# Sample attention of a decoder step: two batches side by side on 128 partitions, token rows kept in DRAM meanwhile

## The reference, cut to what matters

```python
def _sb_attend(q, k, v, mask, sb_bias):
    z = jnp.einsum('bqhd,bkhd->bhqk', q, k) * (q.shape[-1] ** -0.5)
    z = z + sb_bias[None, :, None, None]
    log_1m = jnp.where(mask, jax.nn.log_sigmoid(-z), 0.0)
    excl = lax.cumsum(log_1m, axis=3, reverse=True) - log_1m
    a = jnp.where(mask, jnp.exp(jax.nn.log_sigmoid(z) + excl), 0.0)
    return jnp.einsum('bhqk,bkhd->bqhd', a, v)

def _dilated_sample(q, k_buf, v_buf, rel_bias):
    ...
    for window, dil in DILATED_PATTERNS:     # (128,1), (512,4), (2048,16)
        idx = lb + jnp.arange(t)[:, None] - dil * m[None, :]
        kg, vg = jnp.take(k_buf, idx, axis=1), jnp.take(v_buf, idx, axis=1)
        logits = jnp.einsum('bthd,btmhd->bhtm', q32, kg) * scale + bias.T[:, None, :]
        lse = jax.nn.logsumexp(logits, axis=-1)
        outs.append(jnp.einsum('bhtm,btmhd->bthd', jnp.exp(logits - lse[..., None]), vg))
        ...
    return _combine_dilations(outs, lses)
```

## Time and profile before

| | |
|---|---|
| median of three runs | 2693.51 us |
| span of the profiled execution | 2693.6 us |
| sample attention in it (870.56 to 1733.90 us) | 863.3 us |
| TensorE busy | 2265.2 us, 84% |
| VectorE busy | 1438.1 us, 53% |
| ScalarE busy | 1021.5 us, 38% |
| GpSimd busy | 816.8 us, 30% |
| mean granted TensorE clock | 0.909 |
| moved by DMA | 371.71 MB |

### The profile page before, as it was taken

One profiled execution on the slowest core, in us unless ns is written; L12 is line 12 of the kernel. 1 busy time (PEld: TensorE's weight loads), 2 busy tenths in 40 slices (PEclk: granted clock), 3 DMA queues, 4 the chain that ended last, 5 costly groups with the idle time before them and its releaser, 6 DMA issues. The chain is left out here.

```text
span 2693.6 us, 42705 instructions
## 1 busy us (share of the span) xinstructions
PE 2265.2 (84%) x15058; PEld 2062.9 (77%) x15058; DVE 1438.1 (53%) x1784; ACT 1021.5 (38%) x1582; POOL 816.8 (30%) x401
## 2 busy tenths in 40 slices
PE   5999955776666788888888898577999999999998
PEld 4999934555555677767776776477899999999997
DVE  5111128898986587877787887475522212222213
ACT  3000015767666455556555555421301211111212
POOL 2211104333340254553553543411222221122210
PEclk7999977878888798988898998789999999999999
DMA  3222175212210676666666766510444334433332
GB/s 114 98 85 84 65 280 144 67 47 57 65 48 26 194 242 200 221 212 209 211 212 211 226 203 219 176 36 32 141 141 141 124 109 140 140 128 137 108 124 105
DMA packets 183929, 371.71 MB, mean 138 GB/s; under 512 B 38289, under 2 KB 71442, under 8 KB 182674
## 3 DMA queue, kind: packets, MB, share of 16 engines
q1 hardware_dynamic: 178130, 289.64, 34.2%
q0 software_dynamic: 5056, 79.96, 8.3%
q10 hardware_dynamic: 624, 0.80, 0.2%
HBM read 339.07 MB, written 98.11 MB: 162 GB/s over the span
## 5 line engine op out<-in xcount | busy, mean ns | idle before, releaser
L1406 POOL TENSOR_TENSOR sa_v_lo<-sa_v_in,sa_v_hi 128x1536 fp32r<-128x1536 f32 (+2 forms) x104 | 341.0, 3282 | 436.8 <-ACT sa_v_hi L1602 342.1
L393 POOL TENSOR_TENSOR mlp_w_lo<-mlp_raw,mlp_w_hi 128x2048 fp32r<-128x2048 f32 x30 | 138.2, 4606 | 585.7 <-ACT mlp_w_hi L439 585.7
L1666 DVE TENSOR_TENSOR sa_kT_lo<-sa_kt,sa_kT_hi 128x512 fp32r<-128x512 f32 (+1 forms) x352 | 211.2, 653 | 144.1 <-ACT sa_kT_hi L1564 143.8
L1467 PE MATMUL sa_s<-sa_kT_hi,sa_qd 128*128 128x512 f32 (+1 forms) x704 | 246.4, 414 | 3.7 <-DVE sa_kT_lo L1666 3.7
L552 DVE TENSOR_TENSOR xT<-xT,mlp_acc 128x1088 f32<-128x1088 f32 x64 | 82.4, 1287 | 278.8 <-PE mlp_acc L144 278.8
L962 PE MATMUL pr_turned<-ident,pr_take 128*128 128x128 f32 x576 | 100.2, 306 | 140.2 <-DVE pr_wtsT L1145 127.4
L1444 PE MATMUL sa_kt<-ident,sa_k_in 128*128 128x128 f32 x1344 | 177.3, 289 | 42.6 <-DMA sa_k_in<-in_cache_sb_k 21.6
L1564 ACT ACTIVATE sa_kT_hi<-sa_kt 128x512 fp32r<-128x512 f32 (+1 forms) x352 | 174.9, 570 | 100.2 <-PE sa_kt L1444 100.2
L1444 PEld LDWEIGHTS sa_kt<-ident,sa_k_in 128*128 128x128 f32 x1344 | 166.3, 150 | 55.6 <-DMA sa_k_in<-in_cache_sb_k 22.7
L962 PEld LDWEIGHTS pr_turned<-ident,pr_take 128*128 128x128 f32 x576 | 68.6, 153 | 166.2 <-issue 166.0
L144 PE MATMUL mlp_acc<-n_hi,mlp_w_hi 128*128 128x272 f32 x1024 | 171.8, 290 | 21.0 <-POOL mlp_w_lo L120 16.3
(11 more groups left out here) (193 smaller groups left out, 5237.8 us busy)
## 6 DMA issues: line engine op xcount, KB each, us to landing
sa_k_in<-in_cache_sb_k SPq DMA_DIRECT2D x256, 256.0 KB, 3.5
sa_v_in<-in_cache_sb_v SPq DMA_DIRECT2D x256, 256.0 KB
out<-in_cache_win_k POOLq DMA_DIRECT2D x16, 2040.0 KB, 8.7
out<-in_cache_win_v POOLq DMA_DIRECT2D x16, 2040.0 KB, 8.6
sa_k_in<-in_cache_win_k SPq DMA_DIRECT2D x80, 256.0 KB, 4.3
sa_v_in<-in_cache_win_v SPq DMA_DIRECT2D x80, 256.0 KB
mlp_raw<-in_w_up SPq DMA_DIRECT2D x16, 1024.0 KB, 11.5
mlp_raw<-in_w_down SPq DMA_DIRECT2D x16, 1024.0 KB, 11.0
```

The source lines that it names most:

```text
L393: pool.tensor_tensor(out=ring.lo[:, n % 2, :], in0=ring.raw[:, n % 2, :], in1=ring.hi[:, n % 2, :].bitcast(F32), op=ALU.subtract).then_inc ...
L1406: last = pool.tensor_tensor(out=v_lo[0:rows, h, i, :], in0=v_in[0:rows, s, i, :], in1=v_hi[0:rows, h, i, :].bitcast(F32), op=ALU.subtract)
L1467: last = pe.matmul(out[:, 0:w], qd[:, k, qp, c * P:(c + 1) * P], kT[:, n % 2, c, 0:w], start=(c == 0 and x == 0), stop=(c == PAIRS - 1 and ...
L1666: dve.tensor_tensor(kT_lo[:, n % 2, c, 0:w], kt_ps[:, c, 0:w], kT_hi[:, n % 2, c, 0:w].bitcast(F32), ALU.subtract).then_inc(kT_lo_done, 1)
```

## The change

`sample_stage` now takes two batches at a time (G = 2), four turns in place of eight. Their 2 x 64 rows lie side by side on the 128 partitions of the scores, of the two sigmoids, the scan, the product, the softmax and the transposed weights, so that these are one instruction for two batches. Keys and values of the two batches stay apart: the queries of batch g stand in columns g x 64 of `qd[..., g, ...]`, with zeros elsewhere, and all eight (batch, head pair) products of a unit add up in one accumulator. Values go to one accumulator per batch.

A step, one unit of both batches, is cut into eight slots j (batch j // 4, head pair j % 4). In each slot every engine does one eighth of each kind of work: TensorE transposes the keys of a slot three ahead, scores this slot, and multiplies one tile of values of the unit four steps back. Sigmoids stand in slot 0 of the next step, scan and product in slots 1 and 2, value halves of two tiles in slots 2, 3, 5 and 6, weights in slots 6 and 7 three steps after their scores; `own_heads` and `place` have slots of their own. Key and value buffers are three instead of two, `kT` six slots, `v_hi` and `v_lo` six halves. GpSimd makes all of `v_lo`. The new tokens' keys, before a product of their own, are loaded as eight more rows of a unit; the unit of new tokens alone is now two pages and the new tokens, and the last unit two pages. There are 42 tiles per batch as before.

The tables on 128 partitions take more SBUF. For that `xT` is written to DRAM (`xT_spill`, 4.46 MB) in the input projection and its space given free; the output projection reads it back.

```diff
-    NU, LAG = 12, 4
-    tiles = [4, 4, 2, 0] + [4] * 8
+    G, R = 2, NS
+    NG = B // G
+    SL = G * PAIRS
+    tiles = [4, 4, 2] + [2] + [4] * 7 + [2]
...
-    KS, VS, VH, WS = 2, 2, 3, 5
+    AHEAD = 3
+    KS, KR, VS, VH, WS = 3, 6, 3, 6, 4
...
                 # SyncE
                 def step(b, prev, s):
-                    if b is not None:
-                        load_keys(b, s)
-                    bv, n = unit(b, prev, s - 4)
-                    if bv is not None:
-                        load_values(bv, n)
+                    for g in range(G):
+                        if b is not None:
+                            load_keys(b, s, g)
+                        bv, n = unit(b, prev, s - (LAG - 1))
+                        if bv is not None:
+                            load_values(bv, n, g)
...
+                    for i, (qp, kT) in enumerate(((0, kT_hi), (0, kT_lo), (1, kT_hi))):
+                        last = pe.matmul(out, qd[:, k, qp, g, c * P:(c + 1) * P], kT[:, x % KR, 0:w],
+                                         start=(j == 0 and i == 0), stop=(j == SL - 1 and i == 2 and not masked))
...
                 # TensorE
                 def step(b, prev, s):
-                    if b is not None:
-                        score(b, s)
-                        next_keys(turn_keys, b, s)
...
+                    for j in range(SL):
+                        if b is not None:
+                            turn_keys(*ahead(b, s, j + AHEAD))
+                            score(b, s, j)
+                        if j == 3 and s == LAG and prev is not None:
+                            place(prev, SB)
+                        if j == 3 and s == LAG + 3 and b is not None:
+                            place(b, DIL)
+                        bv, n = unit(b, prev, s - (LAG - 1))
+                        if j == 6 and bv is not None:
+                            turn_weights(bv, n)
+                        bv, n = unit(b, prev, s - LAG)
                         if bv is not None:
-                            do(bv, n)
+                            values(bv, n, j)
...
                 # ScalarE
-                for t in range(TS):
+                for g in range(G * TS):
...
                     act.dma_start(zb[rows, 0:1], sb_bias[0:1, :].rearrange("o h -> h o"),
                     act.dma_start(bias[rows, :], by_distance[:, TS - 1 - t:TS - 1 - t + WIN + TS]).then_inc(bias_in, 16)
...
+                        if j == 0 and bg is not None and kind[n] == SB and not (b is None and s > 0):
+                            gate(bg, n)
+                        if b is not None:
+                            keys_hi(*ahead(b, s, j + AHEAD))
+                            if s == 3 and j == 2:
+                                exponent(b)
...
+                            if j in (2, 3, 5, 6):
+                                values_hi(bw, nw, (2, 3, 5, 6).index(j))
+                            if j == 7:
+                                weights_hi(bw, nw)
...
                 # VectorE
-                def fourth_low(b, n):
...
+                            keys_lo(*ahead(b, s, j + AHEAD))
+                        if bg is not None:
+                            if kind[n] == DIL and j == 0:
+                                dilated(bg, n)
+                            if kind[n] == SB and j == 1:
+                                stayed(bg, n)
+                            if kind[n] == SB and j == 2:
+                                taken(bg, n)
+                        if s == 3 and j == 5 and b is not None:
+                            softened(b)
...
                 # dense_stage: SyncE, then VectorE
                 fetch(0, 1)
+                if spill is not None:
+                    sp.dma_start(spill.rearrange("(c p) t -> p c t", p=P), src[:, :, :]).then_inc(moved, 16)
+                if refill is not None:
+                    sp.dma_start(residual[:, :, :], refill.rearrange("(c p) t -> p c t", p=P)).then_inc(moved, 16)
...
                 dve.wait_ge(inverted, groups)
+                if refill is not None:
+                    dve.wait_ge(moved, 16)
```

More of the change, by code:

```diff
@@ L146, in split_products, with dense_stage @@
     return last
-def dense_stage(nc, cx, tag, weights, src, gain, ones, groups, hi, lo, turns, load=None, store=None, residual=None):
+def dense_stage(nc, cx, tag, weights, src, gain, ones, groups, hi, lo, turns, load=None, store=None, residual=None,
+                spill=None, refill=None):
     PW = 256
@@ L210, in _ @@
                 turn(turns - 1, False)
+                if spill is not None:
+                    sp.wait_ge(moved, 16)
                 if store is not None:
@@ L1397, in queries @@
[L1397 to L1408 removed]
+                    done = b * 8
@@ new lines, in low @@
+                def low(b, n, q):
+                    g, h = q // 2, q % 2
+                    if halves[n][h] is None:
+                        return
+                    p, vs = 4 * n + q, (n * G + g) % VS
+                    t0, t, own_rows = halves[n][h]
+                    pool.wait_ge(v_hi_done, b * NC + through[p])
+                    rows = TS if own_rows else P
+                    t = max(t, 1)
+                    pool.tensor_tensor(out=v_lo[0:rows, p % VH, 0:t, :], in0=v_in[0:rows, vs, t0:t0 + t, :],
+                                       in1=v_hi[0:rows, p % VH, 0:t, :].bitcast(F32), op=ALU.subtract).then_inc(v_lo_done, 1)
@@ L1423, in step @@
                     if bv is not None:
-                        low(bv, n)
+                        for q in range(4):
+                            low(bv, n, q)
                 queries(0, DIL)
@@ L1484, in turn_weights @@
                         pe.wait_ge(sb_weights, b * 9 + n - 2)
[L1485 to L1487 removed]
+                        src = take[:, n % WS, 0:wide[n]]
+                    if n or not no_former(b):
+                        pe.wait_ge(wt_out, b * NU + n)
                     pe.sem_inc(cx.passed, 1)
[L1489 to L1490 removed]
@@ new lines, in turn_weights @@
+                    if n == 1 and not no_former(b):
+                        pe.wait_ge(place_out, b * 2)
+                    if n == 4:
+                        pe.wait_ge(place_out, b * 2 + 1)
+                    t = tiles[n]
+                    for i in range(t):
+                        last = pe.transpose(w_ps[:, i * P:(i + 1) * P], src[:, i * P:(i + 1) * P], ident[:, :])
+                    if new[n]:
+                        last = pe.transpose(w_ps[0:TS, t * P:(t + 1) * P], src[:, t * P:t * P + TS], ident[:, :])
@@ new lines, in place @@
+                def place(b, k):
+                    pe.wait_ge(owned, b * 4 + 2 * k + 2)
+                    pe.wait_ge(wt_out, b * NU + (4 if k == DIL else NU + (0 if isinstance(b, int) and b == NG - 1 else 1)))
+                    for g in range(G):
+                        for c in range(PAIRS):
+                            a = (g * PAIRS + c) * TS
+                            last = pe.matmul(w_ps[:, a:a + TS], o_own[:, g, c * P:(c + 1) * P], tok[:, :],
+                                             start=True, stop=True)
+                    last.then_inc(placed, 1)
@@ L1770 @@
+                for j in range(AHEAD):
+                    keys_lo(0, 0, j)
+                pipeline(dve, step, LAG + 1)
 class Semaphores:
```

640 lines of the change are left out of this document (299 added, 341 removed).

## The result

The changed kernel takes 2553.36 us (median of 4 runs, 2550.85 to 2557.55) against 2692.03 us; the ratio is 0.9487, 95% interval 0.9473 to 0.9502. 2570 us was forecast, in a range of 2515 to 2665. The profiled execution has a span of 2549.3 us at a granted clock of 0.933.

The account below looks back on a forecast made before the run. TensorE was taken as nearly the bound, losing time to gaps and slow clock; setup 32 + TensorE's work 611 + softmax 32 + tail 19 + small stalls 45 = 739 us instead of 863, giving 2570 us, range 2515 to 2665.

Parts of the forecast that it names:

- What bounds: Sample stage before: TensorE nearly the bound, but 22.6 us of each 102.4 us batch lost to gaps and clock.
- wait for `o_own`: TensorE's wait before the placing matmuls, 46.8 us in 15 waits, goes because VectorE makes it several slots ahead.
- Setup: Stage start up to the first transpose: taken as proportional to the DMA pairs of zb and bias, 32 us.
- TensorE's work: Matmuls and transposes of the sample stage hardly change: 611 us for four pairs, against 638 before.
- Softmax: Dilated softmax, once a pair: late key copy and late weights, plus half-clock loss, 4 x 8.1 = 32 us.
- Tail: Last score to next stage: again about 36 us, 17 of them counted as TensorE's work, 19 remain.
- Small stalls: Steps of the stage: scan or product held until a GpSimd instruction ends; 45 us, between zero and 133.
- Engine loads: In a step of 13.8 us: ScalarE about 11, GpSimd 9.9, VectorE below 11 us, so all hidden.
- No small stalls: Rival: stalls in the stage's steps cost 0 to 10 us instead of 45; 2530 us, chance 0.18.
- The lock bound: Rival: VectorE's scans and products held by GpSimd, stalls of 133 us instead of 45; 2658 us, chance 0.16.
- The gaps only move: Rival: TensorE keeps its loss of 181 us in the stage, at other waits; 2673 us, chance 0.10.
- Loads bind: Rival: key and value loads of the stage don't rise above 214 GB/s; 2704 us, slower, chance 0.08.

Follow-up runs that it names:

- zb_first: The changed kernel with the 16 DMAs of zb issued before the 16 of bias instead of alternating with them; 2543.8 us.
- all_four: The changed kernel with zb DMAs first, loop written out, softmax in pieces with its scaling on ScalarE, and query copies moved; 2529.8 us.
- one_batch: The changed kernel's slots, order and leads, but one batch at a time on 64 partitions instead of pairs; 2645.7 us.
- in_blocks: The changed kernel with pairs, but TensorE does all value products of a step first, then the eight slots of keys and scores; 2666.3 us.
- two_buffers: The changed kernel with two buffers each for keys and values instead of three; 2785.7 us.
- both cut-down kernels: one_batch and in_blocks, each the changed kernel without one of its two parts, pairs or interleaving; 2645.7 and 2666.3 us.
- in_blocks_early: As in_blocks, but with the weights turned in slot 4 and copied in slot 5 instead of 6 and 7; 2626.9 us.
- one_batch_early: As one_batch, but weights of all steps but the softmax's turned in slot 0 and copied in slot 1, instead of 2 and 3; 2625.6 us.
- lead2: The changed kernel with keys turned two slots ahead instead of three; 2549.2 us.
- lock_meets: The changed kernel with VectorE's scan and product three slots later, where GpSimd's value halves run; 2580.7 us.

## Why the prediction was right, and where it was not

*What bounds.* Right: the time lay in TensorE's gaps and in the clock behind them, and most of both went, 69 and 64 us. The wait for `o_own` has gone as said.

*Sum.* 739 us was forecast for the stage, 720.2 came. Setup 25.9 instead of 32: it is not proportional to the number of DMA pairs (zb_first). TensorE's work: 615.6 us busy less half of 28.7 are 601, and with the 17 of the tail that the forecast counted 618; forecast 611. It fell by 21 us, 27 forecast. Softmax: 14.4 us of waits and half of the 14.2 us that TensorE was busy at half clock behind the four stops, 21.5 instead of 32; the clock fell for 3.4 us behind three stops and 6.8 behind the fourth. The forecast had a stop of 2.1 us at the key copies and one of 2.6 at the weights; the first came to 0.8 us at most, the second was 2.7 to 4.0 us, with the scaling held up as shown. Tail, 19 forecast, 20.5. Small stalls: the other 26.7 us of idle time and 7.2 of clock, 34 instead of 45. Three terms were forecast too high and two too low, so part of the nearness of the sum is luck.

*The step that failed* is the reason given for the small stalls. They were priced by scans and products that meet GpSimd; no scan met it and few products did, and the waits left are the loop's branch (9.5 us), key loads (12.0) and some 6.4 for value and weight parts. The size came out near by luck: the term was an allowance between two bounds. The lock is where the prediction did not look for it, in the scaling of the softmax. The branch was not in the working at all.

*Engine loads.* A full step without a stop took 13.3 us (13.8 forecast), a pair 168.6 (172), in which ScalarE was busy 110 and GpSimd 111: all hidden, as costed.

*Rivals.* No small stalls (2530 us) is what all_four reaches, not the change. The lock bound costs 27 us where it is made to meet, not the 133 of the rival, since the key chain has time to spare and only weights come late. The gaps only move: idle time and clock together fell from 188 to 55 us, so not in the change; in one_batch and in_blocks much of the loss did stay, part of it in new waits behind the lock. Loads bind: right in its mechanism (two_buffers, 2785.7 us); 259 GB/s were reached where the prediction's estimate for a single 256 KB load, a straight line in time between two sizes, was 130, and no run here has loads one at a time.

## What to carry to other kernels

Price a gap of the bounding engine with the stretch of slow clock behind it, and read both from the trace. When a change has two parts, run each alone, and look at what else each moved: here both cut-down kernels met the lock, and looked 20 to 40 us worse until the weights behind it were made earlier. A wait that is shortened is only gone when the next instruction on that chain is early too.

## What was not expected of the hardware

A gap's price in clock is not fixed. Before, 110 us of idle time came with 178 us at half clock; in in_blocks 125 us came with 88, in in_blocks_early 94 with 55. The length of the gaps does not sort them: the latter two have 82 and 74 gaps over 0.25 us, 1.5 and 1.2 us long in the mean, and one_batch_early, with 33 gaps of 2.3 us, has 94 us at half clock for 78 idle; but lead2, with 26 gaps of 1.3 us, has 57 for 34. Nor is the sum steady: the four runs of the changed kernel have mean clocks from 0.926 to 0.933, by an estimate from these some 36 us at half clock over the whole span, so a difference of 20 us between two profiles says little. What sets the price stays open.

A scaling with one SBUF operand and a column of factors waits for GpSimd as products do: on 64 partitions 0.88 us in the kernel before and 1.80 in one_batch, on 128 partitions 2.54 here. The Trainium skill ("SBUF — State Buffer", section "Who interferes with whom") names such scalings among those that can take the shared port; the trace agrees. The scan waits too: 1.29 us here against 2.24 in lock_meets.
